# A four-layer fp32 network on one NeuronCore: three down projections turned to 512 weight columns past standing activations

## The reference, cut to what matters

```python
# layers 0 and 1, behind the mixer; D_FF = 4096
hn = rmsnorm(h, gains[2])
ff = jnp.square(jax.nn.relu(hn @ w_up[layer])) @ w_down[layer]     # 4096 -> 1024
h = h + rmsnorm(ff, gains[3])                                      # norm over the 1024 features of a token
gate = jax.nn.sigmoid(h @ w_ple_gate[layer])
h = h + gate * (p[layer] @ w_ple[layer])                           # p: 256 tokens x 256
# layers 2 and 3; D_FF_2 = 2816
h = h + gated @ w_down_2[l]                                        # 2816 -> 1024, no norm behind it; layer 3's h is the output
```

## Time and profile before

| | before |
|---|---|
| median of 3 runs | 1508.3 us (1506.88 to 1509.05) |
| the profiled execution | 1507.89 us, span 1506.6 us |
| TensorE busy | 96% (10884 matmuls) |
| VectorE, ScalarE, GpSimd busy | 66%, 51%, 7% |
| mean granted TensorE clock | 0.974 |
| DMA | 228 MB, 151 GB/s on average |

### The profile page before, as it was taken

How to read it: one execution, slowest core, us unless ns; L and a number is a source line. 1 busy time by engine, 2 the same in 40 slices (tenths; PEclk the granted TensorE clock), 3 DMA queues, 4 the chain that set the end, 5 groups by cost and what they waited for, 6 DMA issues and landing times.

```text
span 1506.6 us, 26045 instructions
## 1 busy us (share of the span) xinstructions
PE 1452.7 (96%) x10884; PEld 1378.7 (92%) x10884; DVE 994.2 (66%) x1495; ACT 774.3 (51%) x1219; POOL 108.8 (7%) x100
## 2 busy tenths in 40 slices
PE   7999989999998889999999998999999998999999
PEld 7989989999986789999998788999998788999999
DVE  5575667664687557654486866777756677677763
ACT  6644445444574354443366765544445676644443
POOL 0004111100000001110000000011100000011100
PEclk9999999999999899999999989999999989999999
DMA  8532156556454135655555221655565412265553
GB/s 260 164 112 84 57 165 192 176 177 197 157 197 140 57 112 172 196 172 192 190 162 167 96 84 57 193 168 171 184 195 193 152 57 85 84 186 179 186 185 106
DMA packets 186574, 228.19 MB, mean 151 GB/s; under 512 B 5965, under 2 KB 161229, under 8 KB 186457
## 3 DMA queue, kind: packets, MB, share of 16 engines
q1 hardware_dynamic: 185448, 221.75, 46.0%
q0 software_dynamic: 1008, 4.77, 0.9%
HBM read 225.46 MB, written 1.05 MB: 150 GB/s over the span
## 4 chain that ended last, share of the span: by engine, by line
PE 71%; DVE 18%; ACT 7%; issue 3%; POOL 0%; DMA 0%; ACTq 0%; DVEq 0%; SPq 0%; POOLq 0%
PE bank L495 20%; PE bank L497 19%; PE bank L496 19%; DVE weights_low L786 7%; ACT weights_high L684 3%; PE bank L503 3%; PE bank L1006 2%; PE bank L2052 2%; PE bank L2073 2%; DVE cv L2944 2%; ACT S L2139 2%; DVE cv L2941 1%; DVE S L2200 1%; DVE pad L2931 1%; DVE cv L2950 1%
## 5 line engine op out<-in xcount | busy, mean ns | idle before, releaser
L786 DVE TENSOR_TENSOR weights_low<-weights_raw,weights_high 128x1024 fp32r<-128x1024 f32 (+2 forms) x421 | 507.0, 1226 | 289.0 <-ACT weights_high L684 288.9
L684 ACT CAST weights_high<-weights_raw 128x1024 fp32r<-128x1024 f32 (+2 forms) x421 | 424.6, 1031 | 257.9 <-PE bank L497 256.6
L495 PE MATMUL bank<-hT_high,weights_high 128*128 128x256 f32 x1640 | 471.5, 288 | 10.4 <-DVE hT_low L862 4.8
L496 PE MATMUL bank<-hT_low,weights_high 128*128 128x256 f32 x1640 | 466.6, 285 | 0.0
L497 PE MATMUL bank<-hT_high,weights_low 128*128 128x256 f32 x1640 | 466.4, 284 | 0.0
L495 PEld LDWEIGHTS bank<-hT_high,weights_high 128*128 128x128 f32 x1640 | 316.6, 193 | 16.5 <-issue 9.4
L496 PEld LDWEIGHTS bank<-hT_low,weights_high 128*128 128x128 f32 x1640 | 316.8, 193 | 0.3
L497 PEld LDWEIGHTS bank<-hT_high,weights_low 128*128 128x128 f32 x1640 | 316.5, 193 | 0.2
L495 PE MATMUL bank<-aT_high,weights_high 128*128 128x256 f32 x864 | 241.9, 280 | 0.2
L496 PE MATMUL bank<-aT_low,weights_high 128*128 128x256 f32 x864 | 241.0, 279 | 0.0
L497 PE MATMUL bank<-aT_high,weights_low 128*128 128x256 f32 x864 | 240.8, 279 | 0.0
(11 more groups left out here) (417 smaller groups left out, 1829.8 us busy)
## 6 DMA issues: line engine op xcount, KB each, us to landing
weights_raw<-in_w_up SPq DMA_DIRECT2D x32, 1024.0 KB, 5.4
weights_raw<-in_w_down SPq DMA_DIRECT2D x32, 1024.0 KB, 5.2
weights_raw<-in_ffn_w_gate SPq DMA_DIRECT2D x22, 1024.0 KB, 5.4
weights_raw<-in_ffn_w_up SPq DMA_DIRECT2D x22, 1024.0 KB, 5.3
weights_raw<-in_w_in SPq DMA_DIRECT2D x20, 1024.0 KB, 5.1
weights_raw<-in_w_in_ab SPq DMA_DIRECT2D x16, 1024.0 KB, 5.7
weights_raw<-in_ffn_w_down SPq DMA_DIRECT2D x16, 1024.0 KB, 5.3
weights_raw<-in_w_o SPq DMA_DIRECT2D x10, 1024.0 KB, 5.0
```

The source lines that it names most:

```text
L495: k.E.matmul(out, xh, wh, start=first, stop=False)
L496: k.E.matmul(out, xh, wl, start=False, stop=False)
L684: k.A.copy(w.halves(n)[0], w.raw_part(n)).then_inc(*k.s.weight_high(n))
L786: k.V.tensor_tensor(low, w.raw_part(n), high.bitcast(F32), ALU.subtract).then_inc(*k.s.weight_low(n))
```

## The change

The down projections of layers 0, 1 and 3 use panels of four chunks x 512 columns instead of eight chunks x 256. In each pass 128 tokens of `aT` stand, and 512 weight columns stream past. Two banks (one for each 128 tokens) are filled over half of the features, then two more. Layer 2's stays as it was. The number of panels and of halves doesn't change in layers 0 and 1. In layer 3 the last panel of each half-matrix has two chunks.

In layers 0 and 1 the result now has tokens on the partitions, so the norm's factor is a number per partition. ScalarE squares and sums along the row, with the first half-matrix done mid-way. VectorE scales the first 512 features and ScalarE the last 512. TensorE transposes the result in four sets of four, amid the embedding's product, and VectorE adds each pair with the gain to `h` straight from PSUM. The sums, the spreading of the factor and GpSimd's additions go.

In layer 3 the old `h` is transposed ahead of each half-matrix and copied to the output tile; VectorE adds the bank to it, and it is stored without another transpose.

```diff
+def deep_by_tokens(key, w, chunks):
+    return [panel(key, w, k, min(4, chunks - k), n, 512) for n in range(0, D, 512) for k in range(0, chunks, 4)]
...
-        plan += by_pairs(("down", layer), T["w_down"][layer], DFF1 // P)
+        plan += deep_by_tokens(("down", layer), T["w_down"][layer], DFF1 // P)
...
-        plan += by_pairs(("down_2", l), T["ffn_w_down_2"][l], DFF2 // P)
+        plan += (deep_by_tokens if l else by_pairs)(("down_2", l), T["ffn_w_down_2"][l], DFF2 // P)
...
+def tensor_deep_by_tokens(k, st, n0, x, chunks, key, ready):
+    banks = [k.banks.fill((st, "out", n0, t), hold=True) for t in range(NT)]
+    for k0 in range(0, chunks, 4):
+        n, nk = k.w.first_part[k.w.take(key + (k0, n0))], min(4, chunks - k0) // 2
+        for i in range(2):
+            k.E.wait_ge(*k.s.weight_low.at(n + i))
+            w = k.w.halves(n + i)
+            for t in range(NT):
+                for d in range(nk):
+                    c = k0 + i * nk + d
+                    if n0 == 0 and t == 0:
+                        k.E.wait_ge(*ready(c))
+                    mm = tensor_product(k, banks[t][:, :], half(x, np.s_[:, c, t * P:(t + 1) * P]), half(w, np.s_[:, d, :]), c == 0, c == chunks - 1)
+                keys = ([("half", n + i)] if t else []) + ([(st, "out", n0, t)] if c == chunks - 1 else [])
+                if keys:
+                    mm.then_inc(*k.s.products(*keys))
+    for t in range(NT):
+        k.banks.let_go((st, "out", n0, t))
...
 def scalar_feed_forward_1(k, layer):
+    first = k.w.first(("down", layer, 0, 512))
+    scalar_split(k, first)
+    scalar_half_squares(k, st, m, 0)
+    A.activation(m.post_inv, k.ones[:, 0:NT], ACT.Sqrt).then_inc(*s.root((st, "post begun")))
+    for k0 in range(4, DFF1 // P, 4):
+        scalar_split(k, k.w.first(("down", layer, k0, 512)))
+    last = k.w.first(("ple", layer, 0, 0))
+    scalar_split(k, last - 1)
+    scalar_half_squares(k, st, m, 512)
+    scalar_split(k, last)
+    for t in range(NT):
+        key = (st, "out", 512, t)
+        A.wait_ge(*s.factored.at((st, "post")))
+        A.activation(m.u[:, t, 512:D], k.banks[key][:, :], ACT.Copy, scale=m.post_inv[:, t:t + 1]).then_inc(*k.banks.read(key))
     for p in range(4):
         scalar_residual(k, ("gate", layer), p, st, k.ple[layer].hT, None, False)
...
+def scalar_half_squares(k, st, m, n0):
+    A, s = k.A, k.s
+    for t in range(NT):
+        key = (st, "out", n0, t)
+        A.wait_ge(*s.products.at(key))
+        scalar_square_sum(k, key, k.banks[key][:, :], m.ss[:, n0 // 512, t:t + 1])
+        if n0:
+            A.wait_ge(*s.mean.at((st, "half")))
+            A.wait_ge(*s.squares.last())
+            A.activation(m.post_inv[:, t:t + 1], m.ss[:, 1, t:t + 1], ACT.Sqrt, bias=m.ss[:, 0, t:t + 1], scale=1.0 / D).then_inc(*s.root((st, t)))
...
 def vector_feed_forward_1(k, layer):
+    vector_split(k, last - 1)
+    V.wait_ge(*s.root.at((st, 1)))
+    V.reciprocal(m.post_inv, m.post_inv).then_inc(*s.factored((st, "post")))
+    V.wait_ge(*s.factored.at((st, "post")))
+    for t in range(NT):
+        V.wait_ge(*k.banks.was_read((st, "out", 0, t)))
+        V.tensor_scalar(m.u[:, t, 0:512], m.u[:, t, 0:512], m.post_inv[:, t:t + 1], None, ALU.mult).then_inc(*s.mixed((st, t)))
+    vector_split(k, last)
+    def added(p):
+        key = ((st, "post"), "T", 2 * p)
+        V.wait_ge(*s.products.at(key))
+        for c in (2 * p, 2 * p + 1):
+            op = V.scalar_tensor_tensor(k.h[:, c, :], k.banks[key][:, c % 2 * SEQ:(c % 2 + 1) * SEQ], gain[:, c:c + 1], k.h[:, c, :], ALU.mult, ALU.add)
+        op.then_inc(*k.banks.read(key))
     for p in range(4):
+        added(p)
+        if p:
+            vector_residual(k, ("gate", layer), p - 1, k.ple[layer].hT, None)
+    vector_residual(k, ("gate", layer), 3, k.ple[layer].hT, None)
...
 def tensor_gated_add(k, layer):
-    def post_factor():
-        for _ in range(3):
-            yield
-        tensor_sums_by_token(k, (("ff1", layer), "post"))
-        for _ in range(3):
-            yield
-        tensor_along_tokens(k, (("ff1", layer), "post"), k.ff1[layer].post_inv)
+    def post_turned():
+        fst, u = ("ff1", layer), k.ff1[layer].u
+        for p, steps in enumerate((7, 1, 3, 1)):
+            for _ in range(steps):
+                yield
+            for t in range(NT):
+                E.wait_ge(*(s.mixed.at((fst, t)) if p < 2 else k.banks.was_read((fst, "out", 512, t))))
+            tensor_transposes(k, ((fst, "post"), "T", 2 * p), [u[:, t, (2 * p + i) * P:(2 * p + i + 1) * P] for i in range(2) for t in range(NT)])
...
+def tensor_residual_by_tokens(k, n0):
+    for t in range(NT):
+        tensor_transposes(k, ("residual", n0, t), [k.h[:, n0 // P + i, t * P:(t + 1) * P] for i in range(4)])
+def vector_output(k, n0):
+    for t in range(NT):
+        key, out = (("ff2", 1), "out", n0, t), k.ff2[1].out[:, t, n0:n0 + 512]
+        k.V.wait_ge(*k.banks.was_read(("residual", n0, t)))
+        k.V.wait_ge(*k.s.products.at(key))
+        k.V.tensor_tensor(out, out, k.banks[key][:, :], ALU.add).then_inc(*k.banks.read(key))
```

More of the change, by code:

```diff
@@ L830, in residual_after @@
 def residual_after(k, st, p):
+    if st[0] == "ff1":
+        return k.banks.was_read(((st, "post"), "T", 2 * p))
     return k.banks.was_read((st, "out", p)) if st[0] in ("m2", "ff2") else k.s.residual.at((st, p))
@@ L899, in vector_add_post @@
     first_added(1)
-    if nst[0] == "ff1":
-        vector_residual(k, nst, 0, dst, gain)
-        next(splits, None)
+    vector_residual(k, nst, 0, dst, gain)
+    next(splits, None)
     added(1)
-    if nst[0] != "ff1":
-        vector_residual(k, nst, 0, dst, gain)
     vector_residual(k, nst, 1, dst, gain)
@@ L1713, in tensor_feed_forward_1 @@
     tensor_feature_major(k, ("p", layer), m.pt, 2)
-    for p in range(4):
-        tensor_pair_panels(k, st, p, m.aT, DFF1 // P, ("down", layer), lambda c: s.active.at((st, c - c % 2)))
+    for n0 in (0, 512):
+        tensor_deep_by_tokens(k, st, n0, m.aT, DFF1 // P, ("down", layer), lambda c: s.active.at((st, c - c % 2)))
 def scalar_feed_forward_1(k, layer):
@@ L1729, in scalar_feed_forward_1 @@
     scalar_feature_major(k, ("p", layer), 2, m.pT)
[L1730 to L1734, removed]
+    for k0 in range(0, DFF1 // P, 4):
+        scalar_split(k, k.w.first(("down", layer, k0, 0)) + 2)
+        if layer == 0 and k0 == 16:
             for which in range(2):
@@ L1793, in vector_feed_forward_1 @@
     vector_feature_major(k, ("p", layer), 2, m.pT)
-    for p in range(4):
[L1795 to L1800, removed]
+    for k0 in range(0, DFF1 // P, 4):
+        vector_split(k, k.w.first(("down", layer, k0, 0)) + 2)
+        if layer == 0 and k0 == 8:
+            vector_turn_tables(k)
+    vector_split(k, k.w.first(("down", layer, 0, 512)))
+    for t in range(NT):
+        key = (st, "out", 0, t)
+        V.wait_ge(*s.squares.at(key))
+        V.tensor_copy(m.u[:, t, 0:512], k.banks[key][:, :]).then_inc(*k.banks.read(key))
+    V.tensor_scalar(m.ss[:, 0, :], m.ss[:, 0, :], 1.0 / D, EPS, ALU.mult, ALU.add).then_inc(*s.mean((st, "half")))
+    for k0 in range(4, DFF1 // P, 4):
+        vector_split(k, k.w.first(("down", layer, k0, 512)))
+    last = k.w.first(("ple", layer, 0, 0))
+    vector_split(k, last - 1)
[6 more added lines that the diff above has]
+    vector_split(k, last)
+    gain = post_gain(k, layer, 1)
+    def added(p):
[4 more added lines that the diff above has]
+        op.then_inc(*k.banks.read(key))
+    for p in range(4):
+        added(p)
+        if p:
+            vector_residual(k, ("gate", layer), p - 1, k.ple[layer].hT, None)
+    vector_residual(k, ("gate", layer), 3, k.ple[layer].hT, None)
 def gpsimd_feed_forward_1(k, layer):
@@ L2865, in tensor_feed_forward_2, with scalar_residual_by_tokens @@
         tensor_feature_linear(k, st, ("ff_up", l, 0, n0), m.hT, ("up", n0 // P))
[L2866 to L2883, removed]
+    ready = lambda c: k.s.active.at((st, c - c % 2))
+    if l == 0:
+        for p in range(4):
+            tensor_pair_panels(k, st, p, m.aT, DFF2 // P, ("down_2", l), ready)
+    else:
+        for n0 in (0, 512):
+            tensor_residual_by_tokens(k, n0)
+            tensor_deep_by_tokens(k, st, n0, m.aT, DFF2 // P, ("down_2", l), ready)
+def tensor_residual_by_tokens(k, n0):
+    for t in range(NT):
+        tensor_transposes(k, ("residual", n0, t), [k.h[:, n0 // P + i, t * P:(t + 1) * P] for i in range(4)])
+def scalar_residual_by_tokens(k, n0):
+    for t in range(NT):
+        k.A.wait_ge(*k.s.products.at(("residual", n0, t)))
+        k.A.copy(k.ff2[1].out[:, t, n0:n0 + 512], k.banks["residual", n0, t][:, :]).then_inc(*k.banks.read(("residual", n0, t)))
+def vector_output(k, n0):
+    for t in range(NT):
+        key, out = (("ff2", 1), "out", n0, t), k.ff2[1].out[:, t, n0:n0 + 512]
+        k.V.wait_ge(*k.banks.was_read(("residual", n0, t)))
+        k.V.wait_ge(*k.s.products.at(key))
```

(19 more changed lines are left out.)

26 lines of the change are left out of this document (9 added, 17 removed).

## The result

| | before | after |
|---|---|---|
| median of 9 runs each | 1507.61 us (1506.45 to 1509.05) | 1512.64 us (1506.17 to 1514.3) |
| ratio | | 1.0026, 95% interval 1.0015 to 1.0038 |
| profiled span | 1506.6 us | 1511.4 us |

A forecast was written before the change was run, and what follows sets the result against it. TensorE, busy 96% of the span, was taken as the bound. Terms -6.8 - 0.8 - 1.25 + 3.0 + 2.8 = -3.05 gave 1505.3 us from a median of 1508.3; range 1501.5 to 1514.

The forecast's parts named there:

- stream, layers 0 and 1: Down projections of layers 0 and 1: 512-column passes take 87.15 us against 90.54, -3.4 us each, -6.8 together.
- layer 3's product, with its transposes: Layer 3's down projection: 264 wide passes, four sets of transposes and restarts take 61.45 us against 62.26, -0.8.
- tail: After the last matmul: one addition and the store take 3.2 us instead of 4.45, -1.25.
- bank's turn, without the clock: Before the gate in layers 0 and 1: waiting for the embedding's bank stalls TensorE 3.8 us; +1.5 a layer, +3.0.
- clock: Behind the hole before the gate, layers 0 and 1: half clock for some 3 us costs 1.4 a layer, +2.8.
- I take 226.7, as most stretches have it: 512-column passes in layers 0, 1 and 3: 226.7 ns each, the commoner traced rate, with 234.7 as the other end.
- standing activations that lie elsewhere in SBUF than the norm's output: Rival for the 512-column passes: they keep the slow 234.7 ns, total +5.2, 1513.5 us; chance 0.22.
- rival of a rate between: Rival for the 512-column passes: 4 ns more a pass, some 1509.3 us; chance 0.20, shared with a longer half clock.
- 7.7 us at half speed: Upper end for the clock loss behind each hole before the gate: 7.7 us at half speed, costing 3.4 us.
- the clock is not taken: Rival at the hole before the gate: no half clock follows, 1502.5 us; chance 0.08.
- the bank is no wait: Rival at the hand-over: gate starts at 7.6 us, no clock lost, total -13.2, 1495 us; chance 0.08.
- the mid-way squares, copies and table load cost nothing: Layers 0 and 1, mid down projection: ScalarE's extra work ends some 10 us before its next split is due; nothing.

The follow-up runs named there:

- e3: Changed kernel with 960 bytes put ahead of aT, so it starts at the split weights' position modulo 1024 bytes; 1507.32 us (one run).
- e2: Changed kernel with an empty tile of 64 bytes a partition ahead of aT in all four layers; 1508.5 us (one run).
- e4: Changed kernel with 64 bytes ahead of hT and 64 behind it, moving hT to 960 modulo 1024 from the split weights; 1503.06 us (one run).
- e1: Changed kernel with the PSUM bank turn set back, so the gate takes the transposed sets' banks; 1500.08 us, ratio to before 0.9949.
- e7: Kernel before the change with hT, aT and gate_hT at 960 bytes modulo 1024 from the split weights; 1492.33 us, ratio 0.9899.
- e5: Changed kernel with the bank turn set back and aT at 0 modulo 1024 from the split weights (960 in layer 2); 1489.59 us, ratio 0.9881.
- e6: e5 with hT and gate_hT also at 960 bytes modulo 1024 from the split weights; 1489.11 us, ratio 0.9869.
- e9: e5 with standing aT at 256 (layers 0 and 1) and 512 (layer 3) bytes modulo 1024 from the split weights; 1489.81 us, ratio 0.9879.
- e8: Kernel before with hT at 832, aT at 704 (layers 0, 1), 512 (layer 2), 256 (layer 3) modulo 1024 from the split weights; 1500.36 us (one run).
- e11: Kernel before with aT and gate_hT at 960 modulo 1024 from the split weights, hT left; 1501.54 us over 10 runs, ratio 0.9978.

## Why the prediction was wrong

| term | forecast | measured |
|---|---|---|
| stream, layers 0 and 1 | -6.8 | -1.7 |
| layer 3's product, with its transposes | -0.8 | +0.9 |
| tail | -1.25 | -1.17 |
| bank's turn, without the clock | +3.0 | +2.4 |
| clock | +2.8 | +5.4 |
| elsewhere | 0 | -1.1 |
| sum | -3.05 | +4.7 |

**The stream failed.** The step is "I take 226.7, as most stretches have it". Most stretches were all of one tile, `hT` at place 0; `aT` stands at 64, and ran at 233.3 (233.6 with the first steps). e3 shows the cause by itself: `aT` moved to place 0 and nothing else, and the forecast 87.15 us came out as 87.16. The prediction's rival named it, "standing activations that lie elsewhere in SBUF than the norm's output", and gave it 0.22. It deserved most of the chance: two of the tiles that the trace showed differed, a third one was to be judged, and counting stretches weighed one tile five times. The 5.1 us of this term and the 1.7 of layer 3 are most of the miss of 7.8. By the Trainium skill (TensorE: Matmul & The Clock Gate, Back-to-back issue gap) a merged pair should save 2.5 ns, which the prediction weighed and set aside; here it saved 2 x 117.9 - 233.6 = 2.2. That it fits is luck: at place 0, with 120.0 in e3's layer 2, a pair merged would save 13.3, and the absolute spacings of its formula were met by no place tried. The rival of a rate between puts this rule near 1509.3; worked out from 117.9 it gives 233.3 ns a pass, 6.6 above 226.7, and so 1512.1.

**The clock was half right.** Half clock came, as forecast, but for 5.7 us behind the hole (6.0 in layer 1), not for the 2.9 to 3.4 of the two neighbours. What was lost is 25.26 - 22.62 = 2.64 us and 2.79 in layer 1, not 1.4 each; half of 5.7 and 6.0 is 2.85 and 3.0. The upper end that I kept, 7.7 us at half speed, was the nearer one (half of 7.7 is 3.85, where the prediction has 3.4). It is a term that was mis-sized for this execution. Over the eight holes of the changed kernel, e2, e3 and e4 the loss is 2.05 on average: e2 drew nearly the forecast 1.4, and e4's layer 1 drew the rival "the clock is not taken". One number for each hole was the wrong form for this term.

**The bank was right,** by its mechanism and nearly by its size: the gate 11.14 us behind the mark (11.3 forecast), the hole 3.52 (3.5 to 4), ended by the copy named. The time without clock is +2.46 at the first matmul less the old stalls and their neighbours, 1.27 in the old product, so 1.2 a layer against 1.5. e1 is the rival "the bank is no wait" made true: its 1495 with the stream and layer 3 at the real rate (+5.1, +1.7) is 1501.8, and 1500.1 was measured.

**The tail was right,** and so was the claim that the mid-way squares, copies and table load cost nothing: the down projection after has no hole; the longest step in it is the first, 0.32 us.

## What to carry to other kernels

Take a pass's rate from the same operand in the same role; if the trace has it only for other tiles, treat the tiles, not the stretches, as the sample, and keep the slow end likely. Where work with fewer banks between is put into a round-robin of PSUM banks, list who gets which bank and who must copy it out first; one line that chose the bank was worth 12.6 us here. Then try the tile's place: with the turn mended and `aT` at a multiple of 256 bytes from the split weights, the change that lost 0.26% gains 1.2% (1489.6 against 1507.0). But give the kernel before the same chance ahead of crediting the change: with moved tiles alone it gains 1.0% (e7, 1492.3), and the intervals of the two ratios overlap. What the new form has for sure is steadiness: at place 0 its down projections of layers 0 and 1 took 87.15 or 87.16 us in every profile, where the old form at place 960 took 87.14 or 90.53.

## What the runs showed of the hardware

- The step of a weight load with a 512-column pass goes by the standing tile's place modulo 256. At 0 it is 226.7 ns (`aT` in e3, e5, e6, e9; `hT`), at 64 233.3 (`aT` after, `hT` in e8), at 96 234.3 (`memT`; 233.3 where the moved weights put it at 224, 32 and 160, in e4, e7 and e8), at 128 232.5 (`aT`, e2), at 192 228.9 (`hT`, e4 and e7). Moving tile and weights together changes nothing (`aT` in e4). It isn't quite without exception: in e6 two stretches of 36 passes of `hT` took 8.17 us (233.4 ns), where e7 has 8.01 in the same stage and place, and in e2 one half of layer 3 ran at 233.3. `aT` at place 0 held 226.7 in every stretch but for some 24 passes in e6's layer 3.
- With 256 columns moving past standing weights the step is 120.0 ns at multiples of 256 bytes (`hT` before, `aT` in e3 and e8) and at 96 (`bT` and `pT` before), and 118.6 at 128 (`aT` in e2's layer 2). `pT`, in stretches of only some 24 passes, had 116.7 at 32 (e3, e5, e9) and 118 at 224 (e7, e8). At 64 and 192 it is 113.3 or 117.8. Which of these two, a stretch of hundreds of passes can keep, and another execution of the same program may change. This is why the prediction found 119.1 (117.8 without the stalls) and 114.0 in the same tiles. It may also be a part of why e7's four runs spread over 9.6 us beside 2.4 in seven of the kernel before on that chip; but beside e11 the kernel before spread over 7.4 in thirteen. What draws the level stays open; nothing in the traces marks it. So does the mechanism behind the places: that both operands are read from SBUF at once, in a pattern of 256 bytes, is a guess. `bT`'s 54 steps in the kernel before, first and last pass:

```profile
178.47 0.29 PE L495 MATMUL bank<-bT_high,weights_high 128*128 128x256 f32 x1
...
184.95 0.29 PE L495 MATMUL bank<-bT_high,weights_high 128*128 128x256 f32 x1
```

- A hole of 3.5 us, with dense passes on both sides, was followed by 5.7 and 6.0 us at 1.2 GHz in the changed kernel, in which dense work made nothing up, by 3.4 us in e2's layer 0 (from 1.1 us behind the hole's end), and by none in e4's layer 1.
